# Sums of squares of five feed-forwards: two plain float32 matmuls replaced by two in the dense products' format, and moved into the second chunk

## The reference

```
def rmsnorm(x, w):
    xf = x.astype(jnp.float32)
    y = xf * lax.rsqrt(jnp.mean(xf * xf, axis=-1, keepdims=True) + EPS) * w.astype(jnp.float32)
    return y.astype(x.dtype)

def swiglu(h, w_gu, w_down):
    gate, up = jnp.split(h @ w_gu, 2, axis=-1)
    return (jax.nn.silu(gate) * up) @ w_down

# four times, with D_MODEL 1024 and D_FF 2816:
x = x + 0.5 * swiglu(rmsnorm(x, ffn1_norm[layer]), ffn1_w_gu[layer], ffn1_w_down[layer])
# once, in the third block, with D_FF_2 4096:
hf = rms_norm(x, norm_ffn[i])
x = x + jnp.square(jax.nn.relu(hf @ w_ff1[i])) @ w_ff2[i]
```

## Time and profile before

| | us |
|---|---|
| median of 3 runs | 1603.09 |
| the runs | 1603.09, 1602.15, 2177.66 |
| the profiled execution | 1607.01 |
| its span, first to last instruction | 1605.0 |
| TensorE busy in the span | 1536.2 |
| mean granted TensorE clock | 0.989 of full speed |

### The profile page before, as it was taken

The page is one execution under the profiler, slowest core; times in us unless marked ns, Lnnn a source line. Parts: engine busy times, 40 slices in busy tenths (PEclk is TensorE's granted clock), DMA queues, the critical chain, the costliest instruction groups (busy, mean ns, idle before and its releaser), DMA issues. The chain is left out here.

```text
span 1605.0 us, 36127 instructions
## 1 busy us (share of the span) xinstructions
PE 1536.2 (96%) x15669; PEld 1478.2 (92%) x15669; DVE 1064.6 (66%) x1277; ACT 730.3 (46%) x814; POOL 69.9 (4%) x52
## 2 busy tenths in 40 slices
PE   7999989999999999999998999999997889999998
PEld 6999989878999999999988999999886778999997
DVE  5766487764867547664677766467768776777436
ACT  5443345543534344433446433354565444555333
POOL 2000000100100001000101000021000000100000
PEclk9999999999999999999999999999999999999999
DMA  8665545201556556555533555564320012555552
GB/s 269 189 192 201 185 157 169 96 2 51 183 188 193 200 184 184 183 184 187 181 131 96 182 187 191 185 201 145 120 79 3 3 56 81 184 184 189 202 186 79
DMA packets 155065, 243.26 MB, mean 152 GB/s; under 512 B 9283, under 2 KB 106174, under 8 KB 154814
## 3 DMA queue, kind: packets, MB, share of 16 engines
q1 hardware_dynamic: 154510, 240.63, 45.7%
q10 hardware_dynamic: 432, 0.79, 0.2%
HBM read 240.34 MB, written 1.05 MB: 150 GB/s over the span
## 5 line engine op out<-in xcount | busy, mean ns | idle before, releaser
L2888 DVE TENSOR_TENSOR w_lo<-raw,w_hi 128x2048 fp32r<-128x2048 f32 x225 | 522.9, 2335 | 243.0 <-ACT w_hi L2715 242.1
L2518 PE MATMUL dense_ps<-h_hi,w_hi 128*128 128x256 f32 x2368 | 668.3, 282 | 12.2 <-DVE h_lo L2963 8.6
L2519 PE MATMUL dense_ps<-h_lo,w_hi 128*128 128x256 f32 x2368 | 662.0, 280 | 0.0
L2520 PE MATMUL dense_ps<-h_hi,w_lo 128*128 128x256 f32 x2368 | 662.0, 280 | 0.0
L2715 ACT ACTIVATE w_hi<-raw 128x2048 fp32r<-128x2048 f32 x225 | 428.5, 1913 | 332.6 <-DMA raw<-in_ffn_w_down 116.2
L2518 PEld LDWEIGHTS dense_ps<-h_hi,w_hi 128*128 128x128 f32 x2368 | 450.5, 190 | 18.3 <-issue 17.8
L2519 PEld LDWEIGHTS dense_ps<-h_lo,w_hi 128*128 128x128 f32 x2368 | 447.4, 189 | 0.8 <-issue 0.5
L2520 PEld LDWEIGHTS dense_ps<-h_hi,w_lo 128*128 128x128 f32 x2368 | 448.1, 189 | 0.0
L2520 PE MATMUL dense_ps<-g_hi,w_lo 128*128 128x256 f32 x960 | 266.9, 278 | 0.0
L2518 PE MATMUL dense_ps<-g_hi,w_hi 128*128 128x256 f32 x960 | 266.9, 278 | 0.0
L2519 PE MATMUL dense_ps<-g_lo,w_hi 128*128 128x256 f32 x960 | 266.9, 278 | 0.0
(11 more groups left out here) (554 smaller groups left out, 1750.5 us busy)
## 6 DMA issues: line engine op xcount, KB each, us to landing
raw<-in_ffn_w_gu SPq DMA_DIRECT2D x176, 512.0 KB, 4.6
raw<-in_ffn_w_down SPq DMA_DIRECT2D x88, 512.0 KB, 4.1
raw<-in_w_ff SPq DMA_DIRECT2D x64, 512.0 KB, 4.2
raw<-in_w_in SPq DMA_DIRECT2D x36, 512.0 KB, 4.4
raw<-in_a_w_in SPq DMA_DIRECT2D x32, 512.0 KB, 4.3
raw<-in_a_w_out SPq DMA_DIRECT2D x8, 512.0 KB, 4.0
raw<-in_b_w_in SPq DMA_DIRECT2D x8, 512.0 KB, 4.2
raw<-in_b_w_out SPq DMA_DIRECT2D x8, 512.0 KB, 4.1
```

What stands on the lines that cost most here:

```text
L2518: pe.matmul(o, hi, mh, start=start, stop=False)
L2519: pe.matmul(o, hi, ml, start=False, stop=False)
L2520: return pe.matmul(o, lo, mh, start=False, stop=stop)
L2888: dve.tensor_tensor(w_lo[:, p % SLOTS, :], raw[:, p % SLOTS, :], w_hi[:, p % SLOTS, :].bitcast(F32), ALU.subtract).then_inc(lo_ready, 1)
```

## The change

In the stages ffn0 to ffn4 (`PARTED`) VectorE takes up the two folded blocks: it adds them to one block, splits that in a rounded and a remaining part of type fp32r (`sq_r[:, 2]`, `sq_r[:, 3]`, on the memory of `sq`), and copies `ones` into an fp32r block beside them. TensorE multiplies this copy with the two parts, in the dense format, behind the second `kt` of the second chunk, 24 matmuls into it. ScalarE and VectorE split three pieces in place of two before they turn to `rstd`, and none between the first drain and the next turn; VectorE's new instructions stand between the first and the second of these. mixer_b keeps its sum as it was. In the hybrid stage `s_bd` is cleared before the two copies, and one semaphore serves for both.

```diff
--- before.py
+++ after.py
@@ -211,6 +211,7 @@
     small = fixed.take("small", [P, 64])
     scratch_at = fixed.at
     sq = fixed.take("sq", [P, KD, T])
+    sq_r = Map(nc, scratch_at, fixed.at).take("sq_r", [P, KD, T], F32R)
     rstd = fixed.take("rstd", [P, T])
     full3 = fixed.take("full3", [P, 3, 2, T])
     h_at = fixed.at
@@ -252,6 +253,7 @@
 
     ident = constant("ident")
     ones = constant("ones")
+    ones_r = sq_r[:, 5, 0:P]
     ones_head = constant("ones_head")
     eps_col = cst[:, CONST_AT["tiny"][0]:CONST_AT["tiny"][0] + 1]
 
@@ -282,6 +284,7 @@
     sq_half = sem("sq_half")
     norm_mixed = sem("norm_mixed")
     sq_summed = sem("sq_summed")
+    sum_parted = sem("sum_parted")
     gate_scaled = sem("gate_scaled")
     ss_ready = sem("ss_ready")
     rstd_ready = sem("rstd_ready")
@@ -335,6 +338,7 @@
     SPLIT_AHEAD = LATE_SCALE + ["mixer_a"]
 
 
+    PARTED = [s for s in STAGES if s in ("ffn0", "ffn1", "ffn2", "ffn3", "ffn4")]
     FOLDED = [n for s in STAGES if s in LATE_SCALE for n in ([6, 7] if s == "hybrid" else [NORM[s]])]
     SQ_BEFORE = {}
     count = 0
@@ -1539,7 +1543,7 @@
     c_sq, c_ss, c_rs, c_qk, c_rot, c_qkv, c_vturn = (sem(f"c_{n}") for n in ("sq", "ss", "rs", "qk", "rot", "qkv", "vturn"))
     c_sum, c_shift, c_rank, c_lora, c_lsig, c_g = (sem(f"c_{n}") for n in (
         "sum", "shift", "rank", "lora", "lsig", "g"))
-    r_free, r_dec, r_init, r_zero = sem("r_free"), sem("r_dec"), sem("r_init"), sem("r_zero")
+    r_free, r_dec, r_init = sem("r_free"), sem("r_dec"), sem("r_init")
     r_sqk, r_ssk, r_ssm, r_rk, r_kd, r_pq, r_ex, r_ops = (sem(f"r_{n}") for n in (
         "sqk", "ssk", "ssm", "rk", "kd", "pq", "ex", "ops"))
     r_grm, r_g, r_vturn, r_vtok, r_bkt, r_bktok, r_bonus, r_bv = (sem(f"r_{n}") for n in (
@@ -1855,9 +1859,9 @@
         pool.tensor_copy(xt_raw[:, :, :], over_mid(ident, 8)).then_inc(r_init, 1)
         pool.wait_ge(r_free, 1)
         pool.wait_ge(r_g, 4)
+        pool.memset(s_bd[:, :, :], 0.0)
         pool.tensor_copy(x_r[:, :, :], over_mid(ident, 8))
         pool.tensor_copy(xt_r[:, :, :], over_mid(ident, 8)).then_inc(r_init, 1)
-        pool.memset(s_bd[:, :, :], 0.0).then_inc(r_zero, 1)
 
     def hybrid_act(act, link, narrow, splits):
         load_lora(act)
@@ -2275,7 +2279,7 @@
                 masked(i + 1, 1)
             dve.wait_ge(r_s, i + 1)
             if i == 0:
-                dve.wait_ge(r_zero, 1)
+                dve.wait_ge(r_init, 2)
             whole = small_r[:, 32:40].rearrange("p (d i) -> p d i", d=2)[:, :, i]
             for a in HALVES:
                 last = dve.tensor_tensor(s_bd[a, :, a], D_ps[a, 0, 0:P].rearrange("p (d i) -> p d i", d=2),
@@ -2524,7 +2528,7 @@
                 p0, f0 = PIECE_OF[job], FILL_OF[job]
                 h0 = h_before(stage_of[job])
 
-                def chunk(j, turn, first=False, beside=lambda c, r: None):
+                def chunk(j, turn, first=False, beside=lambda c, r: None, second=False):
                     pair = (f0 + j) % 2
                     pe.wait_ge(dense_drained, f0 + j + 1 + 2 * turn)
                     for r in range(2):
@@ -2542,8 +2546,10 @@
                                              start=kt == 0 and nt % 2 == 0, stop=kt == KD - 1 and nt % 2 == 1)
                             if k < 3:
                                 beside(j, kt)
+                            if second and kt == 1 and stage_of[job] in PARTED:
+                                norm(stage_of[job])
                         last.then_inc(piece_used, 1)
-                        if first and r and stage_of[job] in LATE_SCALE and job != "in2":
+                        if first and r and stage_of[job] == "mixer_b":
                             norm(stage_of[job])
                         beside(j, 4 * r + 3)
 
@@ -2558,7 +2564,7 @@
                     return
 
                 for c in range(2):
-                    chunk(c, 0, first=c == 0)
+                    chunk(c, 0, first=c == 0, second=c == 1)
                 after_two()
                 done = 2
 
@@ -2612,6 +2618,11 @@
 
                 if stage == "ffn0":
                     pe.wait_ge(const_loaded, 16)
+                if stage in PARTED:
+                    pe.wait_ge(sum_parted, PARTED.index(stage) + 1)
+                    pe.matmul(M_ps[:, 0, 0:T], ones_r, sq_r[:, 2, :], start=True, stop=False)
+                    pe.matmul(M_ps[:, 0, 0:T], ones_r, sq_r[:, 3, :], start=False, stop=True).then_inc(ss_ready, 1)
+                    return
                 if stage in LATE_SCALE:
                     pe.wait_ge(sq_summed, 2 * FOLDED.index(NORM[stage]) + 2)
                     pe.matmul(M_ps[:, 0, 0:T], ones, sq[:, 0, :], start=True, stop=False)
@@ -2736,8 +2747,9 @@
                     if lead:
                         act.wait_ge(piece_used, p0 + 2)
                         body(0, 0)
-                        split_hi(0, 0)
-                        ahead[0] += 1
+                        if stage_of[job] not in PARTED:
+                            split_hi(0, 0)
+                            ahead[0] += 1
 
                     def turn(t):
                         for i in range(2):
@@ -2807,7 +2819,7 @@
                 if late:
                     square(0)
                     square(1)
-                    splits(3 if stage == "hybrid" else 2)
+                    splits(2 if stage == "mixer_b" else 3)
                 if stage == "hybrid":
                     for k in range(KD):
                         ins = act.activation(sq_w[:, k, :], xT[:, k, :], ACT.Square, scale=column("final_norm", k))
@@ -2909,8 +2921,9 @@
                     if lead:
                         dve.wait_ge(piece_used, p0 + 2)
                         body(0, 0)
-                        split_lo(0, 0)
-                        ahead[0] += 1
+                        if stage_of[job] not in PARTED:
+                            split_lo(0, 0)
+                            ahead[0] += 1
 
                     def turn(t):
                         for i in range(2):
@@ -2968,7 +2981,14 @@
 
                 n = NORM[stage]
                 name, c0 = NORM_COL[stage]
-                if stage in LATE_SCALE:
+                if stage in PARTED:
+                    splits(1)
+                    dve.wait_ge(sq_summed, 2 * FOLDED.index(n) + 2)
+                    dve.tensor_copy(ones_r, ones)
+                    link(dve.tensor_tensor(sq[:, 1, :], sq[:, 0, :], sq[:, 4, :], ALU.add))
+                    split_act(sq[:, 1, :], sq_r[:, 2, :], sq_r[:, 3, :]).then_inc(sum_parted, 1)
+                    splits(2)
+                elif stage in LATE_SCALE:
                     splits(3 if stage == "hybrid" else 2)
                 if stage == "hybrid":
                     return
```

## The result

The changed kernel takes **1624.63 us** (median of six runs), the kernel before 1606.69 (six runs, the three shown earlier among them): a ratio of **1.0107** with a 95% interval of 1.0067 to 1.0147. Each side has one run near 2200 us, which the medians count and the ratio leaves out. The forecast was 1600.0, with 1604.5 as its upper end. The profiled execution took 1622.39 us, with a span of 1620.3 against 1605.0: 15.3 us more.

What follows compares the result with a forecast made beforehand. TensorE's gapless matmul queue in the feed-forwards was taken as the bound: 4.69 us removed less 1.13 added is 3.56, less 0.44 for ffn0's stall is 3.12; profiled 1603.9, median 1600.0 us, range 1596.0 to 1604.5.

Steps and rivals of the forecast that it cites:

- the sums that come: Second chunk of ffn0 to ffn4: two dense-format matmuls at the dense pace add 0.23 us per stage, 1.13 in all.
- The sums that go: Between first and second chunk of ffn0 to ffn4: removing the plain float32 pairs frees TensorE of 4.69 us together.
- Ready in time: VectorE's four small instructions take 1.7 us (1.0 to 2.4); in ffn1 the sum is ready 1.0 us ahead of need.
- What is queued behind: Later splits delay ffn1's first drain from 427.29 to about 431.4; the third chunk starts at 436.2, so nothing is lost.
- ffn0's stall: In ffn0 rstd comes behind piece 4's split, at 39.76; the third chunk starts about 41.15, giving back 0.44 us.
- The larger stall: Rival: ffn0's path to the third chunk is 1.4 us longer, the gain only 1.7, median 1601.4; chance 0.08.
- the late sum: Rival: TensorE waits for VectorE's four instructions in ffn1 to ffn4; 3.2 us lost if they take 3.5; chance 0.04.
- the pair as long as the old one: Rival: the new sum pair saves nothing itself, only 0.38 us of waits in ffn1 and ffn3 go; median 1602.7; chance 0.03.
- The clock: Rival: shifted mixer waits change TensorE's granted clock, 1.7 us either way, median 1598.3 or 1601.7; chance 0.12.
- The range: Median between 1596.0 and 1604.5 us, the low end from the profiled time's 3.9 above the median; within: 0.96.

Runs made afterwards that it cites:

- three: The changed kernel with a third, unread dense-format matmul ahead of the two sum matmuls in each feed-forward; ratio 1.0116 to the kernel before.
- one: The changed kernel with only the first of the two dense-format sum matmuls, the remaining part left out; ratio 1.0074 to the kernel before.
- swap: The changed kernel with the second and third matmul of every dense triple exchanged, the sum pair kept; ratio 1.0077 to the kernel before.
- tiny_mid: The kernel before, its pair untouched, plus one 16-column float32 matmul 24 matmuls into each feed-forward's second chunk; 0.5% below the kernel before, a repeat 1602.89 us.
- reset: The changed kernel plus one unused 16-column plain float32 matmul right behind the dense-format sum pair; 1594.55 us, ratio 0.9965 to the kernel before.

## Why the prediction was wrong

**The step that failed** is the one on *the sums that come*: "Two matmuls of 256 columns in the dense format, at the dense pace: 0.23 us in each of five stages". Their own cost was right. The changed kernel's timeline of ffn0 shows them at L2623 and L2624, 24 matmuls into the second chunk:

```profile
30.31 0.28 PE L2524 MATMUL dense_ps<-h_hi,w_lo 128*128 128x256 f32 x1
30.42 0.28 PE L2623 MATMUL mixer_ps<-sq_r 128*128 128x256 f32 x1
30.54 0.28 PE L2624 MATMUL mixer_ps<-sq_r 128*128 128x256 f32 x1
30.66 0.28 PE L2522 MATMUL dense_ps<-h_hi,w_hi 128*128 128x256 f32 x1
```

Wrong was what it took for granted: that there is one dense pace, which no neighbour alters. The effect of the exchange on the matmuls around it stands in the prediction's sum at nothing. With the old pair, 9 of 16 later feed-forwards ran fast behind the sums; with the new one, 0 of 8, and counting `three`, `one` and `swap` too, 0 of 20. An estimate from that: 9/16 x 4 x 6.4 us = 14.4 us lost, against some 3 won, so 11.3 net. The profiled spans bear it out: 1618.1 on average for those five kernels, 1606.4 for the four with the old pair, 11.8 apart. The medians differ by 17.9 here and by 10 to 18 in the three groups with one of the slow kernels; what is above 11 or 12 I did not settle.

**The rows already said so.** The pace, 0.1135 us, was read in ffn0 alone. The third feed-forward's row holds 1589 matmuls in 188 us, 0.118 each; by the forecast's pace they would have filled 180 us. One division would have shown a 4% effect beside which every term of the sum is small. The kernel before also shows the trigger. In the first mixer, gate products in the dense format go into another accumulator in mid-stream:

```profile
241.54 0.28 PE L637 MATMUL mixer_ps<-h_hi,ba_hi 128*128 128x256 f32 x1
```

There are 24 of them to 244.3, and the stream around them reads:

```profile
230.00:240.00 10.00, 10.00 (x91) 10.00 (x90) 8.56 (x15) 6.24 (x7) 0.00 (x0) 1.00 0.56 182
245.00:255.00 10.00, 10.00 (x87) 10.00 (x86) 7.86 (x11) 3.71 (x2) 0.00 (x0) 1.00 0.46 156
```

**The other steps**, against the changed trace:

- *The sums that go.* Right. Where the pace is slow on both sides the stage shortened by what was forecast: ffn2 188.18 to 187.56 (0.62; forecast 0.86 - 0.23 = 0.63), ffn3 188.39 to 187.55 (0.84; forecast 1.07 - 0.23 = 0.84). At the fast pace, `tiny_mid`'s ffn1 to ffn3 take 181.70, 181.71 and 182.12, `reset`'s 180.90, 181.40 and 181.41: 0.80, 0.31 and 0.71 less (both have one small matmul), although `reset`'s ffn2 and ffn3 ran some 14 us at the slow pace ahead of the sums, worth 0.5 us each.
- *Ready in time.* VectorE's four instructions, ffn0, and the split behind them:

```profile
25.53 0.23 DVE L2987 CAST sq_r<-cst 128x128 fp32r<-128x128 f32 x1 [0.63 <-POOL sq L2697]
25.68 0.42 DVE L2988 TENSOR_TENSOR sq<-sq 128x256 f32<-128x256 f32 x1
26.13 0.29 DVE L2966 CAST sq_r<-sq 128x256 fp32r<-128x256 f32 x1
26.46 0.43 DVE L2967 TENSOR_TENSOR sq_r<-sq,sq_r 128x256 fp32r<-128x256 f32 x1
```

  They take 25.53 to 26.89 = 1.36 us, forecast 1.7 within 1.0 to 2.4. In ffn1 they end at 429.13, 1.8 us before TensorE comes to the sums at 430.94. TensorE waits for none of the five.
- *What is queued behind.* In ffn1 VectorE's drain begins here,

```profile
433.44 0.68 DVE L3075 TENSOR_TENSOR act<-dense_ps,rstd 128x512 f32<-128x512 f32 x1
```

  6.2 later than before on the kernel's own clock, of which 2.6 is ffn1's later start: 3.5 later in the stage, forecast 431.4 - 427.3 = 4.1. Nobody waited.
- *ffn0's stall.* ScalarE answers to the earlier trace rows:

```profile
35.61 1.92 ACT L2726 ACTIVATE w_hi<-raw 128x2048 fp32r<-128x2048 f32 x1 [12.00 <-DMA raw<-in_ffn_w_gu]
37.54 1.28 ACT L2828 ACT_TABLE_LOAD   x1
38.84 0.47 ACT L2836 ACTIVATE rstd<-mixer_ps,cst 128x256 f32<-128x256 f32 x1
```

  Piece 4 at the same 35.61, rstd done at 39.76 as forecast, the third chunk at 41.22 for 41.15. TensorE idled 1.25 ahead of it, not 0.44: it got there earlier than forecast, since in this execution its granted clock in the window from 15 to 41 us was 1.00, against 0.89 before. The start was right all the same, because VectorE's drain set it, and 0.12 earlier than before. The activation begins 1.30 us behind the table load's start. The Trainium skill (ScalarE: Activation LUTs, What ACT_TABLE_LOAD costs) adds a drain of 1.38 us, 2.66 in all; this trace has none, and the measurement decides.
- *The rivals.* The larger stall, the late sum and the pair as long as the old one didn't occur. The clock did take part in the two profiled executions, by more than the 1.7 us priced. In mixer_a, from 385 us on, it read, before and then after:

```profile
385.00:390.00 5.00, 5.00 (x39) 5.00 (x40) 2.80 (x6) 0.00 (x0) 0.00 (x0) 0.89 0.01 3
385.00:390.00 5.00, 4.59 (x22) 4.33 (x22) 2.03 (x6) 0.00 (x0) 0.00 (x0) 0.50 0.02 3
```

  0.50 is the lower level, 1.2 GHz, and TensorE fell back by 1.4 us there. It lost 1.1 more in mixer_a's first ten microseconds (0.70 against 0.83). In the hybrid stage a wait for GpSimd was 0.9 longer (2.62 against 1.68), and 1.7 more went to the clock behind it (0.66 over 5 us, against 1.00). Most of the mixers' +2.7 and +1.9 is this. The change need not be its reason: over the 19 traces mixer_a takes 204.4 to 209.9 us and the hybrid stage 325.6 to 331.8, and the values of both profiles lie inside.
- *The range.* It leaned on the 3.9 us between the profiled time and the median without asking why equal runs of a program without idle time should differ. More runs of the kernel before spread from 1593 to 1624, nearly five steps of pace, and on a single chip over 22 to 30 us, so a range of 8.5 us was too narrow even for no change.

**Shown and not shown.** Shown by repeated runs: the two paces, what each inserted kind leaves behind, the cost. Not shown: why. Beside the 192 ns loads no record in the trace tells of the engine's state behind a pace. Beginnings of stages and waits turn it either way and I found no rule; nor is the old pair without exception, for in mixer_b, whose pair the change doesn't touch, 3 of 14 streams that came fast turned slow, and 5 of 5 that came slow turned fast.
